# Second products of the decay and learning rates in the key stage: three products of fp32r parts on each half of the rows, in place of one fp32 product

## The reference, cut to what matters

```python
    xw = h + dx * mu[4]
    xa = h + dx * mu[5]
    w_log = -jax.nn.softplus(-(w0 + jnp.tanh(xw @ w1) @ w2).astype(f32)) - 0.5
    decay = jnp.exp(-jnp.exp(w_log))
    a = jax.nn.sigmoid((a0 + (xa @ a1) @ a2).astype(f32))
```

## Time and profile before

| | |
|---|---|
| median of 3 runs | 1162.29 us (1159.83 to 1164.28) |
| the profiled execution's own time | 1163.3 us |
| its span, first to last instruction | 1161.3 us |
| PE busy | 1125.3 us, 97% of the span |
| PEld busy | 887.0 us, 76% |
| DVE busy | 735.8 us, 63% |
| ACT busy | 608.5 us, 52% |
| POOL busy | 465.3 us, 40% |
| mean granted TensorE clock | 0.995 |

### The profile page before, as it was taken

The page is one execution under the profiler, slowest core; times in us unless marked ns, Lnnn a source line. Parts: engine busy times, 40 slices in busy tenths (PEclk is TensorE's granted clock), DMA queues, the critical chain, the costliest instruction groups (busy, mean ns, idle before and its releaser), DMA issues.

```text
span 1161.3 us, 19391 instructions
## 1 busy us (share of the span) xinstructions
PE 1125.3 (97%) x7546; PEld 887.0 (76%) x7546; DVE 735.8 (63%) x1172; ACT 608.5 (52%) x1026; POOL 465.3 (40%) x375
## 2 busy tenths in 40 slices
PE   6999999999999999999999999999999999999998
PEld 5756767878868887777777778878888888867776
DVE  6669996966666466666766484573592334567763
ACT  6867445635655466566555554462211343566563
POOL 2341024556744543333332344444454455532240
PEclk9999999999999999999999999999999999999999
DMA  8912347343173633212212223532333333322111
GB/s 277 282 55 73 85 111 222 101 141 85 46 279 121 190 92 90 73 55 73 73 56 72 63 83 104 165 88 81 105 94 92 107 92 91 91 73 67 61 55 73
DMA packets 191613, 123.03 MB, mean 106 GB/s; under 512 B 27877, under 2 KB 176934, under 8 KB 191142
## 3 DMA queue, kind: packets, MB, share of 16 engines
q1 hardware_dynamic: 188918, 119.27, 35.0%
q10 hardware_dynamic: 2608, 2.56, 0.7%
HBM read 105.03 MB, written 16.78 MB: 105 GB/s over the span
## 4 chain that ended last, share of the span: by engine, by line
PE 39%; issue 24%; POOL 12%; DVE 10%; ACT 1%; DMA 1%; POOLq 0%; ACTq 0%; DVEq 0%; SPq 0%
POOL b_w_lo L676 12%; PE banks L764 9%; PE banks L766 9%; PE banks L765 9%; DVE b_problems L2391 2%; DVE b_sum_squares L2389 2%; PE banks L1424 1%; PE banks L771 1%; PE banks L1024 1%; DVE b_a_lo L2220 1%; DMA b_problems<-d_a 1%; PE banks L1442 1%; DVE b_h_t L2216 1%; PE banks L1414 1%; PE banks L1043 1%
## 5 line engine op out<-in xcount | busy, mean ns | idle before, releaser
L676 POOL TENSOR_TENSOR b_w_lo<-b_w_raw,b_w_hi 128x512 fp32r<-128x512 f32 x296 | 399.9, 1372 | 633.9 <-ACT b_w_hi L1521 633.8
L764 PE MATMUL banks<-b_a_lo,b_w_hi 128*128 128x512 f32 x1232 | 492.4, 400 | 8.1 <-POOL b_w_lo L676 3.8
L766 PE MATMUL banks<-b_a_hi,b_w_lo 128*128 128x512 f32 x1232 | 482.5, 392 | 0.0
L765 PE MATMUL banks<-b_a_hi,b_w_hi 128*128 128x512 f32 x1232 | 481.8, 391 | 0.0
L1521 ACT ACTIVATE b_w_hi<-b_w_raw 128x1024 fp32r<-128x1024 f32 x156 | 165.1, 1058 | 248.4 <-PE banks L766 240.6
L764 PEld LDWEIGHTS banks<-b_a_lo,b_w_hi 128*128 128x128 f32 x1232 | 232.3, 189 | 68.7 <-issue 12.8
L766 PEld LDWEIGHTS banks<-b_a_hi,b_w_lo 128*128 128x128 f32 x1232 | 232.2, 188 | 49.8
L765 PEld LDWEIGHTS banks<-b_a_hi,b_w_hi 128*128 128x128 f32 x1232 | 232.5, 189 | 45.2
L1959 ACT ACTIVATE b_exps<-banks,b_stats 128x128 f32<-128x128 f32 (+3 forms) x64 | 33.2, 524 | 67.4 <-DVE b_stats L2658 67.4
L1861 ACT ACTIVATE b_a_hi<-b_x_t,b_params 128x512 fp32r<-128x512 f32 x47 | 33.2, 718 | 23.3 <-DVE b_x_t L2523 22.9
L2514 DVE SCALAR_TENSOR_TENSOR b_a_lo<-b_x_t,b_params,b_a_hi 128x512 fp32r<-128x512 f32 x32 | 31.1, 987 | 21.9 <-ACT b_a_hi L1861 21.9
(11 more groups left out here) (356 smaller groups left out, 1562.0 us busy)
## 6 DMA issues: line engine op xcount, KB each, us to landing
b_w_raw<-rw_w_in SPq DMA_DIRECT2D x32, 512.0 KB, 4.4
b_w_raw<-da_w_in SPq DMA_DIRECT2D x32, 512.0 KB, 4.0
b_w_raw<-w_in_a SPq DMA_DIRECT2D x32, 512.0 KB, 4.0
b_w_raw<-pe_w_gate SPq DMA_DIRECT2D x16, 512.0 KB, 4.2
d_ple<-b_ple_out SPq DMA_DIRECT2D x16, 256.0 KB, 4.3
b_w_raw<-rw_w_out SPq DMA_DIRECT2D x8, 512.0 KB, 4.4
b_ple_in<-d_ple SPq DMA_DIRECT2D x2, 2048.0 KB, 10.7
b_w_raw<-da_w_out SPq DMA_DIRECT2D x8, 512.0 KB, 3.9
```

What stands on the lines that cost most here:

```text
L676: m = pool.tensor_tensor(WLO[:, u % 2, ks], WRAW[:, u, ks], WHI[:, u % 2, ks].bitcast(F32), ALU.subtract)
L764: pe.matmul(dst, hi, a_lo[:, k_act, :], start=first, stop=False)
L765: pe.matmul(dst, hi, a_hi[:, k_act, :], start=False, stop=False)
L766: return pe.matmul(dst, lo, a_hi[:, k_act, :], start=False, stop=last)
```

## The change

The second products are made like the large ones. `LW2` is cut into `LW2H` and `LW2L`, `LT` into `LTH` and `LTL`, all in fp32r, and each `lora_out` is three products for each half of the rows: high weight by low activation, high by high, low by high, the two halves in turn.

```diff
         def lora_out(j):
             if j == 0:
-                pe.wait_ge(sem("lora_act"), 2)
+                pe.wait_ge(sem("lora_mix"), 2 * NT + 3)
             else:
                 pe.wait_ge(sem("sig_done"), 2 * j)
-            for n, rows_ in enumerate((low, up)):
-                m = pe.matmul(BANK[4 + n], LW2[rows_, j * P:(j + 1) * P], LT[rows_, :], start=True, stop=True)
+            for n, (w, t) in enumerate(((LW2H, LTL), (LW2H, LTH), (LW2L, LTH))):
+                for b, rows_ in enumerate((low, up)):
+                    m = pe.matmul(BANK[4 + b], w[rows_, j, :], t[rows_, :], start=(n == 0), stop=(n == 2))
             m.then_inc(sem("z_mm"), 1)
...
+            if j == 3:
+                act.preload_act_table_set("sigmoid_and_others")
+                act.wait_ge(sem("lora_in"), 64)
+                act.wait_ge(sem("small_done"), 6)
+                for n in range(4):
+                    act.wait_ge(sem(f"ple_out{n}"), 32)
+                act.activation(LW2H, LW2[:, :].rearrange("p (j d) -> p j d", d=P), ACT.Copy).then_inc(sem("lora_act"), 1)
             if j >= 4:
                 if j == 4:
 
                     act.wait_ge(sem("lora_mm"), NT)
                     act.activation(LT[0:CH, :], BANK[6][0:CH, :], ACT.Tanh).then_inc(sem("lora_act"), 1)
-                    act.activation(LT[CH:P, :], BANK[6][CH:P, :], ACT.Copy).then_inc(sem("lora_act"), 1)
+                    act.activation(LTH[CH:P, :], BANK[6][CH:P, :], ACT.Copy).then_inc(sem("lora_act"), 1)
+                    act.wait_ge(sem("lora_act"), 3)
+                    act.activation(LTH[0:CH, :], LT[0:CH, :], ACT.Copy).then_inc(sem("lora_act"), 1)
...
         for j in range(NT):
             own.step(tt(DX[:, j, :], H[:, j, 0:TOK], H[:, j, 1:TOK + 1], ALU.subtract))
+        for n in range(4):
+
+            dve.wait_ge(sem(f"ple_out{n}"), 32)
+        dve.wait_ge(sem("lora_act"), 1)
+        tt(LW2L, LW2[:, :].rearrange("p (j d) -> p j d", d=P), LW2H.bitcast(F32), ALU.subtract).then_inc(sem("lora_mix"), 1)
+        dve.wait_ge(sem("lora_act"), 3)
+        tt(LTL[CH:P, :], BANK[6][CH:P, :], LTH[CH:P, :].bitcast(F32), ALU.subtract).then_inc(sem("lora_mix"), 1)
+        dve.wait_ge(sem("lora_act"), 4)
+        tt(LTL[0:CH, :], LT[0:CH, :], LTH[0:CH, :].bitcast(F32), ALU.subtract).then_inc(sem("lora_mix"), 1)
         dve.wait_ge(sem("lora_mm"), NT)
         for k in range(NT):
             mixed(NKX[:, 1, k, :], MU_R, k).then_inc(sem("mix_done"), 1)
```

More of the change, by code:

```diff
@@ L279, in emit @@
     RK = SIG[:, 0, :]
+    LTS = place("lora_t_split", [P, 2, TOK], F32R, x_at)
+    LTH, LTL = LTS[:, 0, :], LTS[:, 1, :]
+    LW2S = place("lora_w2_split", [P, NT, TT, P], F32R, arena + FULL)
+    LW2H, LW2L = LW2S[:, :, 0, :], LW2S[:, :, 1, :]
     (MV,) = over(x_at, [("mix_v", [P, NT, TOK])])
@@ L2267, in _ @@
         dve.wait_ge(sem("tables_in"), 64)
-        for n in range(4):
-            dve.wait_ge(sem(f"ple_out{n}"), 32)
         def scan(j):
```

## The result

| | before | changed |
|---|---|---|
| median, 20 runs each | 1161.3 us | 1168.45 us |
| lowest to highest | 1157.4 to 1164.3 | 1163.6 to 1174.5 |
| profiled execution, own time and span | 1163.3, 1161.3 us | 1170.55, 1168.6 us |
| mean granted TensorE clock, profiled execution | 0.995 | 0.990 |

The ratio is 1.0064, 95% interval 1.0053 to 1.0075: the change made the kernel slower, by 7.4 us (6.2 to 8.7). The forecast was +3.1. The profile after shows two places. The first is where the prediction looked; the second is 270 us later.

The account below looks back on a forecast made before the run. PE was taken to bound that half of the key stage, DVE the receptance stage. Wait +2.8, products -1.1 and clock +1.4 gave +3.1 us, 1165.4 us on the median 1162.29; range 1161.2 to 1168.6.

Parts of the forecast that it names:

- The products: Each `lora_out` on PE takes 1.22 us instead of 1.38, gaining 0.16 each, 1.1 us up to `lora_out(6)`.
- Weight loads on the same rows are not hidden: Rival: rounds two and three of each `lora_out` each wait 0.18 us more; +5.6 us in all, 1167.9; chance 0.05.
- the halves run one behind the other: Rival: the two 64-row halves of each `lora_out` do not overlap; +7.9 us in all, 1170.2; chance 0.06.
- The wait of `lora_out(0)`: In slot 4, PE stands 2.8 us for DVE's three new subtractions, queued behind all eight differences.
- neighbours overlap by a little: DVE's three subtractions overlap slightly, so they end at 66.55 us, not 66.67.
- The clock: After PE's idle time at `lora_out(0)`, the granted clock falls to 0.50, more likely than not; +1.4 us.
- I take the shift of `lora_out(6)` as the shift of the whole: PE's shift at `lora_out(6)`, in slot 7, arrives whole at DVE's list at 99.03 us and passes into the recurrence.
- Transfers, POOL and SP are as before. The sum on PE: These are unchanged; PE's total is +2.8 - 1.1 = +1.7 us before any clock fall.
- A later stage that gives the delay back: Sign of being wrong: DVE reaches the end of the receptance stage less late than its start.
- a dearer round: Rounds of `lora_out` products costing more than forecast; the range's upper end, 3.2 us above the forecast, leaves room for this.

Follow-up runs that it names:

- e4: Changed kernel with the second products in fp32 again, two per output tile; splits, subtractions and PE's wait kept; ratio 1.0045 to the kernel before, +5.2 us.
- e6: Changed kernel with DVE's three subtractions moved among the eight differences and the 2 MB transfer issued after `b_ple_in` landed; ratio 1.0002 to the kernel before, +0.2 us.
- e2: Kernel before with eight tiny fp32 products (32 PE instructions) added ahead of PE's first large product; ratio 1.0069 to the kernel before, +8.0 us.
- e3: Changed kernel with the 2 MB transfer into `b_bonus_v` issued only when `b_ple_in` has landed; ratio 1.0031 to the kernel before, +3.6 us.
- e9: e1 with two rounds per output tile, the weights' low-part product left out; PE instruction count as before; ratio 1.0000 to the kernel before, 0.0 us.
- e1: Changed kernel with DVE's three subtractions moved forward among the eight differences; ratio 1.0040 to the kernel before, +4.6 us.

## Why the prediction was wrong

- **The products: right.** 1.22 us from neighbour to neighbour was forecast, 1.21 is measured, and the weight loads of rounds two and three, on the same rows as the products before them, are hidden: the three rounds together take 0.90 us (88.22 to 89.12). "Weight loads on the same rows are not hidden" and "the halves run one behind the other" are out. The Trainium skill's rule in "TensorE: Matmul & The Clock Gate", Part 3 ("What overlaps and what doesn't") disagrees with line 898 as it did with line 1330.
- **The wait of `lora_out(0)`: right in kind, 0.6 too small.** The three subtractions end 2.70 us behind the differences (62.83 to 65.53; "neighbours overlap by a little" did not hold for them), and PE came 0.4 us earlier relative to DVE than before. The idle time is 3.38 where 2.8 was forecast.
- **The clock: right that it falls, too small in its cost.** One low stretch at a cost of 1.4 us was forecast. In e4 there is one, and it costs 1.55; in the changed kernel the clock was low for two, 6.83 us, at a cost of 2.44. This term was mis-sized by 1.0 us.
- **"I take the shift of `lora_out(6)` as the shift of the whole": wrong for a gain.** A delay goes through (3.40 us at 102.43). A gain does not go through whole, because DVE in front of the receptance stage is nearly full as well: 1.09 on PE became 0.52 on DVE (e6). In the changed kernel, too, PE is 2.83 us late at that point and DVE 3.40: some 0.6 of the 1.1 us that the products gave is not passed on.
- **The step that failed above all is the sum itself.** "Transfers, POOL and SP are as before. The sum on PE" stops at the key stage, and gives the 16 more matmuls and 16 more weight loads no price beyond their own time. They moved the edge of an instruction block by 32 instructions to a place where PE arrives before the block does. e2, e3 and e9 show this from three sides: the count alone makes the gap, a transfer moved away removes it, the old count removes it. Gap and clock are worth 4.4 us by the medians (e1 against e6) and 5.1 in the trace of the changed kernel (2.2 to 7.3 us). No rival had it. "A later stage that gives the delay back" was named as a danger, a later stage that adds to it was not.

The parts add up: e6 +0.2, the first place 3.4 (e3 less e6), the second 4.4 (e1 less e6), together 8.0 against 7.4 measured. Each has an uncertainty of about 3 us, so the split between the two is only rough. In the trace of the changed kernel the first place makes 4.6 us (DVE goes from 1.2 earlier to 3.4 later; 3.1 was forecast) and the second 5.1.

The median, 1168.45, lies just inside the forecast's range, whose upper end is 1168.6. That is luck: the range was made wide there for the scatter of the runs and for a dearer round, and the rounds cost what was forecast.

Not settled: whether the gap sometimes comes in the kernel before. In its profile the instruction packet moved between 331.2 and 332.4 us, and PE, counted in its instructions, came to that edge at 334.3 us, in the sums of line 1175. In it, e4 and e9, which have the same count, the packet starts 2.8 to 3.1 us before PE is at the edge; in the changed kernel, e1 and e2 it starts some 1.2 us after. How large this margin is in other executions no run shows. Nor does any run show what a version would be worth in which DVE could take the whole gain of the products; none of those tried beats the kernel before by more than can be told.

## What to carry to other kernels

Where PE runs through hundreds of short instructions while large transfers are under way, the number of instructions can be a cost of its own: a change far ahead can move a block's edge into such a place, so look for PE gaps put down to "issue" behind a weight load that has already run, and move the transfer. Operands that PE newly waits for are to be made early on the engine that makes them, since the clock added 1.55 us to a wait of 2.8 us here (e4) and 2.44 to one of 3.4 (changed kernel). And before a gain on one engine is counted, the next engine's row has to show idle time that it can fill.

## What the runs showed of the hardware that was not expected

- An instruction packet of 16 KB came 3.3 us later where 2 MB of data were under way behind `b_ple_in` than where they were not, and PE was idle for 3.4 to 3.7 us (changed kernel, e1, e2). In the changed kernel no such packet moved in the 7.5 us from 326.0, with the data queue at 89% of the transfer engines. The Trainium skill's page "Runtime: NRT & Kernel Launch", section "Instruction fetch mechanics", says that instructions come in blocks of 16 KiB (256 instructions) through a queue of the sequencer's own, and that crossing a block's edge is mostly hidden. The packet size and some 252 matmuls and loads to a packet agree; that it is hidden does not hold at this place.
- Products of 64 rows in fp32r run two at a time: six of them and their six loads take 0.90 us, three rounds, where a product on all 128 rows takes 0.23.
- The three rounds' loads, 184 ns each in the records, cost nothing to be seen:

```profile
L898 PEld LDWEIGHTS banks<-b_lora_t_split,b_lora_w_split x48: 182/184/334, 65.6 to 96.2; 64*128 64x128 f32 x48
```

- The clock was 0.50 for 3.4 us somewhere from 113 to 125 us in every profile with the fp32r products (changed kernel, e1, e3, e6, e9), at PE's wait for DVE's `b_w_lo`, and in none of the others. That wait is 2.3 to 2.4 us in these five and 1.8 us in the others: PE comes to it some 0.6 us earlier relative to DVE. In e6 DVE stays 0.52 us ahead of the kernel before from 99 to 181 us, so this fall cost nothing there: DVE sets the pace in that stage.
